# Two softmax attentions of a Trainium2 kernel: unscaled probabilities are multiplied, and a pair's outputs are scaled once

## The chip, the core and the metric

One NeuronCore of a Trainium2 chip runs the whole program in a single launch. The metric is the device time of a launch in microseconds; the median over three runs is compared. All matrix products and tiles are fp32 (128 partitions; TensorE writes to PSUM banks of 128x512 fp32).

## What is computed

The program is three transformer layers over 512 tokens of width 1024. Each of the first two has an attention with 12 token heads and 4 heads over 256 memory rows, all of width 64. The change touches the softmax attentions of these two layers:

```python
# layer 0: windowed attention with a sink
s = einsum('bqkgd,bskd->bkgqs', q_blk, k_blk) * scale + bias
s = where(valid, s, NEG)
p = softmax(concatenate([s, sink_l], axis=-1), axis=-1)[..., :SPAN]
out = einsum('bkgqs,bskd->bqkgd', p, v_blk)
# layer 1: neighbourhood attention on an 8 x 64 grid
s = einsum('bwhd,brwchd->bhwrc', q_row, k_nb) * scale + bias
p = softmax(s.reshape(B, B_HEADS, GRID_W, kr * kc), axis=-1)
out = einsum('bhwrc,brwchd->bwhd', p, v_nb)
# both layers, behind their 12 heads: memory attention
s = einsum('bshd,bmhd->bhsm', q, mk) * HEAD_DIM ** -0.5
p = softmax(s, axis=-1)
out = einsum('bhsm,bmhd->bshd', p, mv)
```

The output goes through a dense projection (`w_out`), a norm and an MLP. The third layer has other attentions; its dilated one runs through the same functions as "phase 2" and keeps its form.

## The kernel before

Every engine has its own program, written out by hand in plain loops; they meet at semaphores only. The order in which an engine works is the order of its code, and a wait holds back all that stands behind it on that engine.

The attention of phase 0 (layer 0) and phase 1 (layer 1) is a list of 32 steps: 8 pairs of heads (6 pairs of token heads, 2 of memory heads), for each pair 4 tiles of 128 queries. A step has two halves, one for each head. A window step has 257 or 385 columns (256 or 384 keys and one for the sink), in the order 257, 385, 385, 257 within a pair; a grid step has 192, 256, 256, 192; a memory step 256. I call the pairs window, grid and memory pairs.

The engines run a software pipeline over s, the number of the step:

- TensorE (`softmax` in its program, L2067): scores of step s into two of four banks (L2095); then `turn` (L2044) transposes the probabilities of step s-3 into one pair of banks, in pieces of 64x128 (8 transposes for 2 blocks of keys, 12 for 3; L2061); then the products with the values of step s-4 (L2139), which add up 128 columns of the pair's output bank. That bank, 64 rows a head and 512 queries, is full behind the fourth step. Scores wait for the masks of step s-2, `turn` for ScalarE's copy of the turn before.
- VectorE (L1260): the mask and row minimum of step s (L1301, two instructions and their accumulator reads), which needs the scores; then, for step s-1, it waits for the exponentials, takes the reciprocals of the two row sums (L1318, 128x2) and multiplies both halves of the probabilities in place (L1323). At the end of a pair it writes `o_lo`, the remainder of the output behind ScalarE's rounded `o_hi` (L1277), one iteration after that cast.
- ScalarE (L847): the copy of the turned probabilities of step s-3 from PSUM to `pt_short` (`copy_turned`, L816, L823), the exponentials of step s with their row sums (`exps`, L826, L834), and at the end of a pair the cast of the output bank to `o_hi` (`copy_output`, L838, L845).
- GpSimd loads the bias tiles of the pairs two pairs ahead, behind the masks that read the old ones.

In the first steps TensorE also makes part of the values, and behind step 31 (`n` is 32) it fills its waits with the first matmuls of the output projection (`begin_out`). The order of these three bodies is what sets the order of the work around the change: there is no scheduler. Banks 4 and 5 (`turn_banks`) take the transposes, banks 6 and 7 the outputs of alternating pairs.

## Time and profile before

| | us |
|---|---|
| median of 3 runs (1914.45 to 1915.96) | 1915.92 |
| the profiled execution | 1916.02 |
| its span | 1914.2 |
| TensorE busy | 1896.0 (99%) |
| VectorE busy | 963.2 (50%) |
| ScalarE busy | 772.5 (40%) |
| GpSimd busy | 182.6 (10%) |

The span is the time from the first to the last instruction on the core; the profiled execution's own time is 1.8 us more. Durations in the rows are those of this one execution. In rows, PE is TensorE (PEld its weight loads), DVE is VectorE, ACT is ScalarE, POOL is GpSimd, SP the engine that issues most loads. Neighbouring instructions of an engine overlap at their ends by some tens of nanoseconds, so the distance from start to start is shorter than a duration. Phase 0 lies at about 84 to 150 us of the span, phase 1 at about 672 to 742.

### The profile page before, as it was taken

The numbers are of one execution on the slowest core, as the hardware profiler recorded it, in microseconds if no ns is written. First come the engines' busy times: TensorE is split into PE (matmuls) and PEld (weight loads), VectorE is DVE, ScalarE is ACT, GpSimd is POOL, SyncE is SP. The second block draws the span as 40 slices with busy tenths as digits, with TensorE's granted clock in tenths as the row PEclk, the third lists the DMA queues.
The fourth block names the chain that finished last, engine by engine and source line by source line (L and its number), as shares of the span: only waits on it lengthen the run. The fifth ranks groups of instructions, "written<-read, shape, count | busy, mean of one in ns | idle before, by whom it ended". The sixth has DMA issues, their size and how long they took to land.

```text
span 1914.2 us, 25105 instructions
## 1 busy us (share of the span) xinstructions
PE 1896.0 (99%) x10458; PEld 1566.7 (82%) x10458; DVE 963.2 (50%) x1497; ACT 772.5 (40%) x1251; POOL 182.6 (10%) x196
## 2 busy tenths in 40 slices
PE   9999999999999999999999999999999999999998
PEld 7878888888888867888888888878887888888887
DVE  5693665553245274566553236443655555325532
ACT  5494433333333285433323324333764443212321
POOL 4112200000005041300000103000000020000000
PEclk9999999999999999999999999999999999999999
DMA  6512233334333311223333332331212333233222
GB/s 191 197 35 77 78 99 99 96 93 143 92 106 117 99 46 56 88 91 97 99 99 91 102 105 99 99 111 57 61 37 86 116 90 97 99 99 97 92 98 88
DMA packets 54136, 182.96 MB, mean 96 GB/s; under 512 B 6604, under 2 KB 10060, under 8 KB 53512
## 3 DMA queue, kind: packets, MB, share of 16 engines
q1 hardware_dynamic: 51528, 172.28, 28.6%
q0 software_dynamic: 2352, 9.02, 1.6%
q8 instruction: 83, 1.36, 0.3%
q14 instruction: 29, 0.24, 0.0%
q10 hardware_dynamic: 144, 0.06, 0.0%
HBM read 176.58 MB, written 4.76 MB: 95 GB/s over the span
## 4 chain that ended last, share of the span: by engine, by line
PE 88%; ACT 4%; DVE 4%; issue 1%; DMA 1%; POOL 1%; SPq 0%; DVEq 0%; ACTq 0%
PE bank L1889 22%; PE bank L1891 22%; PE bank L1890 22%; PE bank L1908 2%; PE bank L1909 2%; PE bank L1910 2%; ACT prob_long L834 1%; PE bank L2139 1%; ACT pt_short L823 1%; PE bank L1669 1%; PE bank L1672 1%; PE bank L1677 1%; PE bank L1968 1%; PE bank L1967 1%; PE bank L1969 1%
## 5 line engine op out<-in xcount | busy, mean ns | idle before, releaser
L1141 DVE TENSOR_TENSOR w_lo<-w_raw,w_hi 128x1024 fp32r<-128x1024 f32 (+3 forms) x319 | 388.2, 1219 | 710.4 <-ACT w_hi L647 710.2
L647 ACT CAST w_hi<-w_raw 128x1024 fp32r<-128x1024 f32 (+3 forms) x319 | 321.9, 1010 | 552.2 <-DMA w_raw<-in_w_down 131.6
L1889 PE MATMUL bank<-h_hi,w_hi 128*128 128x512 f32 x1272 | 496.4, 390 | 0.8 <-DVE w_lo L1141 0.5
L1890 PE MATMUL bank<-h_lo,w_hi 128*128 128x512 f32 x1272 | 495.7, 390 | 0.0
L1891 PE MATMUL bank<-h_hi,w_lo 128*128 128x512 f32 x1272 | 495.7, 390 | 0.0
L1889 PEld LDWEIGHTS bank<-h_hi,w_hi 128*128 128x128 f32 x1272 | 239.2, 188 | 52.9 <-issue 2.2
L1891 PEld LDWEIGHTS bank<-h_hi,w_lo 128*128 128x128 f32 x1272 | 239.2, 188 | 50.2
L1890 PEld LDWEIGHTS bank<-h_lo,w_hi 128*128 128x128 f32 x1272 | 239.1, 188 | 49.3
L1889 PE MATMUL bank<-a_hi,w_hi 128*128 128x512 f32 (+1 forms) x676 | 261.5, 387 | 0.0
L1890 PE MATMUL bank<-a_lo,w_hi 128*128 128x512 f32 (+1 forms) x676 | 261.3, 387 | 0.0
L1891 PE MATMUL bank<-a_hi,w_lo 128*128 128x512 f32 (+1 forms) x676 | 261.3, 386 | 0.0
L1891 PEld LDWEIGHTS bank<-a_hi,w_lo 128*128 128x128 f32 x676 | 127.0, 188 | 25.9
L1889 PEld LDWEIGHTS bank<-a_hi,w_hi 128*128 128x128 f32 x676 | 127.0, 188 | 25.9 <-DVE a_lo L1542 0.3
L1890 PEld LDWEIGHTS bank<-a_lo,w_hi 128*128 128x128 f32 x676 | 127.0, 188 | 25.8
L536 POOL COPY sq_sum<-sq 128x512 f32<-128x512 f32 x6 | 4.1, 685 | 1047.8 <-ACT sq L686 1047.8
L937 ACT CAST a_hi<-raw 128x512 fp32r<-128x512 f32 x44 | 27.3, 621 | 133.8 <-DVE raw L1424 133.8
L539 POOL TENSOR_TENSOR sq_sum<-sq_sum,sq 128x512 f32<-128x512 f32 x35 | 50.4, 1440 | 263.4 <-ACT sq L686 263.4
L834 ACT ACTIVATE prob_long<-prob_long,low_stat 128x256 f32<-128x256 f32 (+3 forms) x128 | 66.0, 527 | 7.0 <-DVE low_stat L1301 6.8
L934 ACT ACTIVATE act_out<-act_out 128x512 f32<-128x512 f32 x44 | 27.8, 632 | 92.8 <-DVE act_out L1419 92.8
L1419 DVE TENSOR_TENSOR act_out<-bank,rstd 128x512 f32<-128x512 f32 x44 | 48.5, 1103 | 11.8 <-ACT rstd L702 11.7
L1101 ACT CAST a_hi<-raw 128x512 fp32r<-128x512 f32 x32 | 19.9, 621 | 83.9 <-DVE raw L1583 83.9
L1908 PE MATMUL bank<-h_hi,w_hi 128*128 128x512 f32 x128 | 52.5, 410 | 0.0
(328 smaller groups left out, 2550.5 us busy)
## 6 DMA issues: line engine op xcount, KB each, us to landing
w_raw<-in_w_gu SPq DMA_DIRECT2D x87, 512.0 KB, 3.5
w_raw<-in_w_mlp_in SPq DMA_DIRECT2D x32, 512.0 KB, 3.5
w_raw<-in_w_mlp_out SPq DMA_DIRECT2D x32, 512.0 KB, 3.6
w_raw<-in_w_down SPq DMA_DIRECT2D x32, 448.0 KB, 3.3
w_raw<-in_w_out SPq DMA_DIRECT2D x24, 512.0 KB, 3.5
w_raw<-in_w_down SPq DMA_DIRECT2D x16, 512.0 KB, 3.5
w_raw<-in_w_gates SPq DMA_DIRECT2D x16, 512.0 KB, 3.5
w_raw<-in_w_qk_b SPq DMA_DIRECT2D x14, 512.0 KB, 3.6
```

The costliest lines, as they stand in the source:

```text
L539: made = nc.gpsimd.tensor_tensor(sq_sum[:, :], sq_sum[:, :], sq[:, c % 2, :], ALU.add)
L647: nc.scalar.copy(hi_of(v), raw_of(v)).then_inc(w_hi_done, 1)
L834: nc.scalar.activation(part, part, ACT.Exp, bias=top, scale=-1.0, accum_out=sums[:, s % 4, half, k:k + 1]).then_inc(p_exp, 1)
L934: nc.scalar.activation(act_out[:, p, :], act_out[:, p, :], ACT.Silu).then_inc(act_done, 1)
L1141: nc.vector.tensor_tensor(lo_of(v), raw_of(v), hi_of(v).bitcast(F32), ALU.subtract).then_inc(w_split, 1)
L1419: nc.vector.tensor_tensor(dst, of, reordered(layer, raw[:, p, :], rstd[:, :])[1], ALU.mult).then_inc(acc_read_dve, 1)
L1889: mm(acc, w1, hi, start=start, stop=False)
L1890: mm(acc, w1, lo, start=False, stop=False)
L1891: last = mm(acc, w2, hi, start=False, stop=end)
L1908: mm(ps[7][:, :], w1, hi, start=c == 0, stop=False)
L1909: mm(ps[7][:, :], w1, lo, start=False, stop=False)
L1910: last = mm(ps[7][:, :], w2, hi, start=False, stop=c == DC - 1)
```

## The change

Four things change in phases 0 and 1:

1. The transposes wait for the exponentials alone (`p_exp`), and what is transposed and multiplied with the values is not normalised. VectorE's reciprocals of 128x2 and its multiplications of the probabilities are gone from these phases.
2. Every row sum of a pair lands at a place of its own. Behind the exponentials of a pair's fourth step VectorE takes one reciprocal of 128x512, in which each of the eight sums (four query tiles, two heads) is read 64 times over, into the tile `raw`.
3. With the transposes of the next pair's first step TensorE transposes these reciprocals too (8 more), so that they lie as the output does; ScalarE's copy of that turn takes 8 blocks, 1024 columns, in place of 4. A turn and a copy of the reciprocals alone stand behind the last step (d == 32).
4. ScalarE's cast of the output is gone. VectorE, five steps later (s = d + 5, d the fourth step of the pair), behind the masks of step s and behind the reciprocal of the pair that has just ended, multiplies the output bank by the turned reciprocals into `act_out`, casts this to `o_hi`, and subtracts for `o_lo`, each waiting for the one before.

```diff
@@ -443,6 +442,13 @@
         attention = [window_steps(), grid_steps(), dilated_steps()]
 
         pt_bufs = [pt_short, pt_short, pt_dil]
+        def turned_blocks(phase, d, steps):
+
+            begin, end = 0, 2 * len(steps[d].blocks) if d < len(steps) else 4
+            if phase < 2 and d and d % 4 == 0:
+                begin, end = 0 if d < len(steps) else 4, 8
+            return begin, end
+
         LAG_T, LAG_V, PROB_RING = (3, 3, 2), (4, 4, 3), (4, 4, 3)
 
         def prob_of(phase, s, half):
@@ -816,10 +822,12 @@
             def copy_turned(phase, d, steps):
                 if d >= 2:
                     act.wait_ge(pv_done, pv[0] + d - 1)
+                if phase < 2 and d % 4 == 2 and d > 2:
+                    act.wait_ge(o_scaled, scaled[0] + d // 4)
                 act.wait_ge(t_ready, turned[0] + 1)
-                n = 2 * len(steps[d].blocks)
-                dst = pt_of(phase, d)[:, :P * n].rearrange("p (n r q) -> p r n q", n=n, r=2)
-                src = turn_banks[:, :, :64 * n].rearrange("p r (n q) -> p r n q", n=n)
+                begin, end = turned_blocks(phase, d, steps)
+                dst = pt_of(phase, d)[:, P * begin:P * end].rearrange("p (n r q) -> p r n q", n=end - begin, r=2)
+                src = turn_banks[:, :, 64 * begin:64 * end].rearrange("p r (n q) -> p r n q", n=end - begin)
                 nc.scalar.activation(dst, src, ACT.Copy).then_inc(pt_copied, 1)
                 turned[0] += 1
 
@@ -831,17 +839,16 @@
                     for k, both in enumerate(st.pieces):
                         p = both[half]
                         part = prob_of(phase, s, half)[:, p["at"]:p["at"] + p["width"]]
+                        of = st.pair_no % 2 if phase < 2 else k
                         nc.scalar.activation(part, part, ACT.Exp, bias=top, scale=-1.0,
-                                             accum_out=sums[:, s % 4, half, k:k + 1]).then_inc(p_exp, 1)
+                                             accum_out=sums[:, s % 4, half, of:of + 1]).then_inc(p_exp, 1)
                 masked[0] += 2 * m
 
             def copy_output(phase, d, steps, o_hi):
                 if not steps[d].last:
                     return
                 act.wait_ge(pv_done, pv[0] + d + 1)
-                dst, src = o_hi[:, steps[d].pair, :], bank_in(phase, 6 + steps[d].pair_no % 2)[:, :]
-                if phase == 2:
-                    dst, src = unclassed(dst, src)
+                dst, src = unclassed(o_hi[:, steps[d].pair, :], bank_in(phase, 6 + steps[d].pair_no % 2)[:, :])
                 nc.scalar.copy(dst, src).then_inc(o_hi_done, 1)
 
             def softmax(phase, o_hi, beside=None, last_values=None, read=None):
@@ -853,12 +860,10 @@
                     if s == 2 and last_values:
                         values_by_tile(last_values, *read)
                     if phase < 2:
-                        if 0 <= s - LAG_T[phase] < n:
+                        if 0 <= s - LAG_T[phase] <= n:
                             copy_turned(phase, s - LAG_T[phase], steps)
                         if s < n:
                             exps(phase, s, steps[s])
-                        if 0 <= s - LAG_V[phase] < n:
-                            copy_output(phase, s - LAG_V[phase], steps, o_hi)
                         if last_values and s >= n:
                             hi_to(last_values[1] + 2 + min(s - n, 2))
                     else:
@@ -1268,12 +1275,21 @@
                         return
                     st = steps[d]
                     o_count[0] += 1
+                    acc = bank_in(phase, 6 + st.pair_no % 2)[:, :]
+                    if phase < 2:
+                        dve.wait_ge(pt_copied, turned[0] + d + 2)
+                        dve.wait_ge(pv_done, pv[0] + d + 1)
+                        o = act_out[:, st.pair_no % 2, :]
+                        nc.vector.tensor_tensor(o, acc, pt_of(phase, d + 1)[:, 4 * P:8 * P], ALU.mult).then_inc(o_scaled, 1)
+                        dve.wait_ge(o_scaled, o_count[0])
+                        nc.vector.tensor_copy(o_hi[:, st.pair, :], o).then_inc(o_hi_done, 1)
+                        dve.wait_ge(o_hi_done, o_count[0])
+                        nc.vector.tensor_tensor(o_lo[:, st.pair, :], o, o_hi[:, st.pair, :].bitcast(F32),
+                                                ALU.subtract).then_inc(o_ready, 1)
+                        return
                     dve.wait_ge(o_hi_done, o_count[0])
-                    dst, src = o_lo[:, st.pair, :], bank_in(phase, 6 + st.pair_no % 2)[:, :]
-                    lead = o_hi[:, st.pair, :].bitcast(F32)
-                    if phase == 2:
-                        lead = unclassed(lead, src)[0]
-                        dst, src = unclassed(dst, src)
+                    lead = unclassed(o_hi[:, st.pair, :].bitcast(F32), acc)[0]
+                    dst, src = unclassed(o_lo[:, st.pair, :], acc)
                     nc.vector.tensor_tensor(dst, src, lead, ALU.subtract).then_inc(o_ready, 1)
 
                 for s in range(n + LAG_V[phase]):
@@ -1306,21 +1322,21 @@
                                 masked[0] += 1
                     d = s - 1
                     if 0 <= d < n:
-                        m, i = len(steps[d].pieces), d % 4
-                        expd[0] += 2 * m
-                        dve.wait_ge(p_exp, expd[0])
-                        total = sums[:, i, :, 0]
-                        if m > 1:
-                            nc.vector.tensor_reduce(den[:, i, :], sums[:, i, :, :m], axis=AX.X, op=ALU.add).then_inc(den_done, 1)
-                            dens[0] += 1
-                            dve.wait_ge(den_done, dens[0])
-                            total = den[:, i, :]
-                        nc.vector.reciprocal(rden[:, i, :], total).then_inc(rden_done, 1)
-                        rdens[0] += 1
-                        dve.wait_ge(rden_done, rdens[0])
-                        for half in range(2):
-                            part = prob_of(phase, d, half)[:, :steps[d].width]
-                            nc.vector.tensor_scalar(part, part, rden[:, i, half:half + 1], None, ALU.mult).then_inc(p_ready, 1)
+                        expd[0] += 2
+                        if phase < 2 and steps[d].last:
+                            dve.wait_ge(p_exp, expd[0])
+                            of = steps[d].pair_no % 2
+                            total = sums[:, :, :, of:of + 1].rearrange("p i h o -> p (i h) o").to_broadcast([P, 8, HD])
+                            nc.vector.reciprocal(raw[:, of, :].rearrange("p (n d) -> p n d", n=8), total).then_inc(rden_done, 1)
+                            rdens[0] += 1
+                        elif phase == 2:
+                            dve.wait_ge(p_exp, expd[0])
+                            nc.vector.reciprocal(rden[:, d % 4, :], sums[:, d % 4, :, 0]).then_inc(rden_done, 1)
+                            rdens[0] += 1
+                            dve.wait_ge(rden_done, rdens[0])
+                            for half in range(2):
+                                part = prob_of(phase, d, half)[:, :steps[d].width]
+                                nc.vector.tensor_scalar(part, part, rden[:, d % 4, half:half + 1], None, ALU.mult).then_inc(p_ready, 1)
                     if phase < 2:
                         output_remainder(s - LAG_V[phase] - 1)
                         if last_values and s >= n:
@@ -1333,9 +1349,10 @@
                         read(s, ps[7], beside.after(s))
                 if phase < 2:
                     output_remainder(n - 1)
-                turned[0] += n
-
-            masked, expd, dens, rdens, o_count, turned = [0], [0], [0], [0], [0], [0]
+                turned[0] += n + 1 if phase < 2 else n
+                pv[0] += n
+
+            masked, expd, rdens, o_count, turned, pv = [0], [0], [0], [0], [0], [0]
 
             def bias_load(phase, pair, half):
 
@@ -2045,14 +2062,14 @@
 
                 if d == 0:
                     wait_reads((act_read, 0, 0))
-                if not 0 <= d < len(steps):
+                if not (0 <= d < len(steps) or phase < 2 and d == len(steps)):
                     return
-                blocks = steps[d].blocks
                 if turned[0]:
                     pe.wait_ge(pt_copied, turned[0])
-                for half in range(2):
+                for half in range(2 if d < len(steps) else 0):
+                    blocks = steps[d].blocks
                     ready[0] += 1
-                    pe.wait_ge(p_ready, ready[0])
+                    pe.wait_ge(p_exp if phase < 2 else p_ready, ready[0])
                     first_key = steps[d].pieces[0][half]["first_key"]
                     for kt, (first, w) in enumerate(blocks):
                         keys = slice(first_key + first, first_key + first + w)
@@ -2061,12 +2078,21 @@
                             last = nc.tensor.transpose(ps[4 + part][:w, at_:at_ + 64],
                                                        prob_of(phase, d, half)[rows(part), keys],
                                                        ident[rows(part), 64 * part:64 * part + 64])
+                if phase < 2 and d and d % 4 == 0:
+                    pe.wait_ge(rden_done, heads[0] + d // 4)
+                    for i in range(4):
+                        for part in range(2):
+                            last = nc.tensor.transpose(ps[4 + part][:, 256 + 64 * i:256 + 64 * i + 64],
+                                                       raw[rows(part), (d // 4 - 1) % 2, P * i:P * i + P],
+                                                       ident[rows(part), 64 * part:64 * part + 64])
                 last.then_inc(t_ready, 1)
                 turned[0] += 1
 
             def softmax(phase, beside=None, rhs=None, after=None, last_values=None, st_out=None):
                 steps = attention[phase]
                 n = len(steps)
+                if phase == 2:
+                    ready[0] = 0
                 if last_values:
                     us, hi, lo, tiles, reads = last_values
                     begin_side()
@@ -2118,9 +2144,10 @@
                             wait_reads((n_act[0], 0, 0))
                         copied[0] += 1
                         pe.wait_ge(pt_copied, copied[0])
-                        banks = 1 if phase == 2 else 2
-                        if st.first and st.pair_no >= banks:
-                            pe.wait_ge(o_ready, heads[0] + st.pair_no - banks + 1)
+                        if st.first and phase < 2 and st.pair_no >= 2:
+                            pe.wait_ge(o_scaled, heads[0] + st.pair_no - 1)
+                        elif st.first and phase == 2 and st.pair_no:
+                            pe.wait_ge(o_ready, heads[0] + st.pair_no)
                         n_v = len(st.vs[0])
                         for x in range(n_v):
                             for half in range(2):
@@ -2151,6 +2178,8 @@
                     if phase == 2:
                         turn(phase, s - LAG_T[phase], steps, n_act[0])
                 heads[0] += steps[-1].pair_no + 1
+                if phase < 2:
+                    copied[0] += 1
 
             scored, ready, turned, copied, heads = [0], [0], [0], [0], [0]
 
```

VectorE's order in phase 0 before (L1301 is the mask, ISA its name here; a pair's last two steps and the next pair's first ones):

```order
L1318 RECIPROCAL rden<-sums 128x2
L1323 TENSOR_SCALAR prob_long<-prob_long,rden 128x385 x2
L1301 ISA prob_long,low_stat<-bank,bias_window 128x257
L1301 ISA low_stat 128x1
L1301 ISA prob_long,low_stat<-bank,bias_window 128x257
L1301 ISA low_stat 128x1
L1318 RECIPROCAL rden<-sums 128x2
L1323 TENSOR_SCALAR prob_long<-prob_long,rden 128x257 x2
L1277 TENSOR_TENSOR h_lo<-bank,h_hi 128x512
L1301 ISA prob_long,low_stat<-bank,bias_window 128x385
L1301 ISA low_stat 128x1
```

The same place after the change (L1317 is the mask, L1330 the reciprocal, L1283 to L1287 the output of the pair before):

```order
L1317 ISA prob_long,low_stat<-bank,bias_window 128x257
L1317 ISA low_stat 128x1
L1317 ISA prob_long,low_stat<-bank,bias_window 128x257
L1317 ISA low_stat 128x1
L1330 RECIPROCAL raw<-sums 128x512
L1283 TENSOR_TENSOR act_out<-bank,pt_short 128x512
L1285 CAST h_hi<-act_out 128x512
L1287 TENSOR_TENSOR h_lo<-act_out,h_hi 128x512
L1317 ISA prob_long,low_stat<-bank,bias_window 128x385
L1317 ISA low_stat 128x1
```

The small reciprocals and multiplications between masks are gone, and once in four steps four instructions of 512 columns stand in a row ahead of the masks of 385 columns.

ScalarE's order around the end of a pair, before (L823 the copy of a turn, with its blocks of 64 as the third number; L834 the exponentials):

```order
L834 ACTIVATE prob_long,sums<-prob_long,low_stat 128x385 x2
L823 ACTIVATE pt_short<-bank 128x2x4x64
L834 ACTIVATE prob_long,sums<-prob_long,low_stat 128x257 x2
L845 CAST h_hi<-bank 128x512
L823 ACTIVATE pt_short<-bank 128x2x6x64
L834 ACTIVATE prob_long,sums<-prob_long,low_stat 128x257 x2
```

And after:

```order
L843 ACTIVATE prob_long,sums<-prob_long,low_stat 128x385 x2
L831 ACTIVATE pt_short<-bank 128x2x8x64
L843 ACTIVATE prob_long,sums<-prob_long,low_stat 128x257 x2
L831 ACTIVATE pt_short<-bank 128x2x6x64
L843 ACTIVATE prob_long,sums<-prob_long,low_stat 128x257 x2
```

The copy ahead of the pair's last exponentials is twice as wide, and the cast behind them is gone.

TensorE's order at the same place after the change (L2078 the transposes of probabilities, L2085 those of reciprocals, L2166 the products with the values, L2121 the scores); before, the row of L2085 is not there and the rest stands as it does:

```order
L2121 MATMUL bank<-k_buf,q_buf 128x256 x2
L2078 MATMUL bank<-ident,prob_long 128x64 x8
L2085 MATMUL bank<-ident,raw 128x64 x8
L2166 MATMUL bank<-pt_short,v_buf 64x128 x4
L2121 MATMUL bank<-k_buf,q_buf 128x256 x2
```

The eight transposes of reciprocals lie between a pair's ordinary transposes and the products with the values.

## Rows read from the trace of the kernel before

**Rows 1.** The page's busy times: us, share of the span, instructions

```profile
PE 1896.0 (99%) x10458; PEld 1566.7 (82%) x10458; DVE 963.2 (50%) x1497; ACT 772.5 (40%) x1251; POOL 182.6 (10%) x196
```

**Rows 2.** Timeline, ScalarE, one window pair: start us, us, what, [idle before]

```profile
102.46 0.58 ACT L845 CAST h_hi<-bank 128x512 fp32r<-128x512 f32 x1
102.92 0.82 ACT L823 ACTIVATE pt_short<-bank 128x768 f32<-128x768 f32 x1
...
104.61 0.81 ACT L823 ACTIVATE pt_short<-bank 128x768 f32<-128x768 f32 x1
105.30 0.63 ACT L834 ACTIVATE prob_long<-prob_long,low_stat 128x385 f32<-128x385 f32 x1
...
106.50 0.60 ACT L823 ACTIVATE pt_short<-bank 128x512 f32<-128x512 f32 x1
...
109.64 0.59 ACT L845 CAST h_hi<-bank 128x512 fp32r<-128x512 f32 x1
```

**Rows 3.** Timeline, ScalarE: casts that bound the six periods, and two grid steps

```profile
144.46 0.58 ACT L845 CAST h_hi<-bank 128x512 fp32r<-128x512 f32 x1
...
689.56 0.56 ACT L845 CAST h_hi<-bank 128x512 fp32r<-128x512 f32 x1
...
715.00 0.50 ACT L834 ACTIVATE prob_long<-prob_long,low_stat 128x256 f32<-128x256 f32 x1
...
715.99 0.58 ACT L823 ACTIVATE pt_short<-bank 128x512 f32<-128x512 f32 x1
716.47 0.45 ACT L834 ACTIVATE prob_long<-prob_long,low_stat 128x192 f32<-128x192 f32 x1
...
717.34 0.57 ACT L845 CAST h_hi<-bank 128x512 fp32r<-128x512 f32 x1
...
730.01 0.59 ACT L845 CAST h_hi<-bank 128x512 fp32r<-128x512 f32 x1
```

**Rows 4.** Timeline, VectorE and ScalarE: masks, remainder, who follows whom

```profile
104.48 0.55 DVE L1301 CUSTOM_DVE_ANT_0 prob_long<-bank,bias_window 128x385 f32<-128x385 f32 x1
...
705.41 0.67 DVE L1277 TENSOR_TENSOR h_lo<-bank,h_hi 128x512 fp32r<-128x512 f32 x1
706.00 0.41 DVE L1301 CUSTOM_DVE_ANT_0 prob_long<-bank,bias_grid 128x256 f32<-128x256 f32 x1
706.34 0.08 DVE L1301 DVE_READ_ACCUMULATOR2_ANT low_stat<- 128x1 f32 x1
...
706.45 0.51 ACT L834 ACTIVATE prob_long<-prob_long,low_stat 128x256 f32<-128x256 f32 x1 [0.61 <-DVE low_stat L1301]
...
730.16 0.17 DVE L1318 RECIPROCAL rden<-sums 128x2 f32<-128x2 f32 x1 [0.46 <-ACT prob_long L834]
```

**Rows 5.** Timeline, TensorE, one narrow step of a window pair

```profile
107.01 0.70 PE L2095 MATMUL bank<-k_buf,q_buf 64*128 64x256 f32 x4
107.54 0.41 PE L2061 MATMUL bank<-ident,prob_long 64*128 64x64 f32 x8
107.88 0.66 PE L2139 MATMUL bank<-pt_short,v_buf 128*64 128x128 f32 x8
108.47 0.49 PE L2095 MATMUL bank<-k_buf,q_buf 64*128 64x256 f32 x2
```

**Rows 6.** Groups by form, VectorE: operation, shapes, count | busy us, mean ns

```profile
L1277 DVE TENSOR_TENSOR h_lo<-bank,h_hi 128x512 fp32r<-128x512 f32 x16 | 10.9, 683 | 5.2 <-ACT h_hi L845 5.2
...
L1318 DVE RECIPROCAL rden<-sums 128x2 f32<-128x2 f32 x72 | 11.5, 160 | 0.9 <-ACT prob_long L834 0.8
...
L1497 DVE CAST sb_ql<-zero_bias 64x512 fp32r<-64x512 f32 x2 | 0.8, 422 | 0.1
...
L1365 DVE CAST neg_tri<-raw 128x128 fp32r<-128x128 f32 x1 | 0.2, 205 | 0.0
```

**Rows 7.** Timeline, TensorE, tail of phase 0: two turns

```profile
145.88 0.46 PE L2061 MATMUL bank<-ident,prob_long 64*128 64x64 f32 x8
...
147.10 0.46 PE L2061 MATMUL bank<-ident,prob_long 64*128 64x64 f32 x8 [0.16 <-ACT pt_short L823]
```

7 lines of the change are left out of this document (4 added, 3 removed).

## The prediction

> **What bounds the kernel now.** I read the page first: TensorE is busy 99% of the span [rows 1], so a microsecond lost or won on TensorE anywhere is one in the total. That average says nothing of the two attentions that the change touches, so next I read the timeline there, engine by engine. I call E the moment at which the exponentials of a pair's last step end; ScalarE then casts the output of the pair before, so each E is the start of a cast and can be read off.
>
> In the first attention, ScalarE's cast starts at 102.46 and again at 109.64 [rows 2]: 7.18 us for a pair of window heads, with no idle entry on any row between. ScalarE sets this period. The six periods from 102.46 to 144.46 take 42.00 us [rows 2, 3]. In the second attention the six from 689.56 to 730.01 take 40.45 us, 6.74 us each, though ScalarE's own work for a grid pair is 4 x 0.48 + 2 x 0.99 + 2 x 0.87 + 0.46 = 6.10: there it also waits for VectorE, as the row at 706.45 shows [rows 3, 4]. From start to start on ScalarE: two exponentials of 257 or 256 columns take 0.99 us, of 385 columns 1.20, of 192 columns 0.87, a copy of turned probabilities 0.48 for 512 columns and 0.69 for 768, the cast 0.46 [rows 2, 3].
>
> TensorE is close behind. A narrow step takes 1.46 us (107.01 to 108.47), of it 0.53 scores and 0.34 eight transposes [rows 5]: 5.84 us for four. VectorE has the masks, the reciprocals, the normalising and the remainder, and is nearly as full. So three engines are balanced, and what counts is less how much each has to do than in which order.
>
> **The change, part by part.** VectorE loses, in each of 64 steps, a reciprocal of 0.16 us and two multiplications of the probabilities. Since ScalarE sets the period in the first attention, this is worth nothing there; in the second it removes some waits of ScalarE.
>
> ScalarE loses 16 casts of 0.46 us and gains 16 copies that are 512 columns wider. From 512 to 768 columns the step grows by 0.21 [rows 2], so to 1024 by 0.42, and the copy takes 0.90 (no such copy of this stage is in the trace; the growth is a straight line between the two that are). Net zero.
>
> TensorE gains eight transposes per pair, 0.34 us, 16 times: 5.4 us of work. It lies under ScalarE's and VectorE's waits if these decide, and on the path if not. The wide copy also delays the next transposes. A turn with 512 columns behind it comes back after 1.22 us (145.88 to 147.10 [rows 7]); with 0.34 and 0.42 more, 1.98, while TensorE has 1.46 + 0.34 = 1.80 of other work. That would be a wait of 0.18 per pair.
>
> VectorE gains four operations per pair, and here the order decides. Once in four steps it waits for E, then runs in a row the reciprocal of 128x512, the multiplication that reads the bank, the cast, and the remainder. Only then come the masks of the next step, though their scores have long been ready, and ScalarE needs these masks for its next exponentials. The chain from E to those exponentials:
>
> - E to VectorE's start: 0.15 (730.01 to 730.16) [rows 3, 4].
> - Reciprocal of 512 columns: not in the trace. Bounds for the forecast are 0.42 below, what a one-input cast of 512 columns took, and 0.68 above; rival 1 takes up what lies far above. I take 0.68, what one 128x512 operation at one element a step costs (the remainder, 0.683) [rows 6]; 0.60 from start to start, since the remainder of 705.41 is followed at 706.00 [rows 4].
> - Multiplication reading the bank: 0.68, the same shape as the remainder, and 0.04 for the semaphore (0.03 at 706.42 to 706.45 [rows 4]).
> - Cast from SBUF to SBUF: 0.42 (0.422 for the same shape [rows 6]; at one element a step it would be 0.68, the upper bound), and 0.04.
> - Remainder: 0.60 to the next start.
> - First mask to its exponentials: 0.45 with 256 columns (706.00 to 706.45), 0.14 more with 385 (0.55 against 0.41) [rows 4].
>
> Sum: 2.98 us, 3.12 for window heads. Without the wait, ScalarE would come to these exponentials after one copy, two exponentials and one copy: 0.48 + 0.87 + 0.48 = 1.83 us behind E in the grid pairs, 1.95 in the memory pairs, 0.69 + 0.99 + 0.69 = 2.37 in the window pairs. So ScalarE stands still for 0.7 to 1.15 us in each pair, on exactly the work that was moved off it.
>
> From there to the next E ScalarE works without a gap: window 1.20 + 0.48 + 1.20 + 0.90 + 0.99 = 4.77; grid 0.99 + 0.48 + 0.99 + 0.90 + 0.87 = 4.23; memory 0.99 + 0.48 + 0.99 + 0.90 + 0.99 = 4.35. New periods: window 3.12 + 4.77 = 7.89, grid 2.98 + 4.23 = 7.21, memory 2.98 + 4.35 = 7.33. Each is longer than TensorE's own (5.84 + 0.34 + 0.18 = 6.36 for narrow pairs), so the added transposes lie under it.
>
> Each attention has six such periods: outputs of six pairs are scaled before the last masks, the other two behind them. First attention: 4 x 7.89 + 2 x 7.33 = 46.22 against 42.00, +4.2. Second: 4 x 7.21 + 2 x 7.33 = 43.50 against 40.45, +3.05. The first wide copy comes before the first of these periods, +0.4 in the first attention. In the tails, eight transposes more (+0.34 each) stand against a wide copy and exponentials that now lie beside the output projection's first matmuls; I take the two at -0.2 together, with bounds of -1.2 and +0.7. The pair's last remainder comes some 0.5 us later than now, under the projection's matmuls that TensorE has in hand.
>
> Waits that the change adds and that I cost at nothing: the transposes of the reciprocals wait for the reciprocal, issued three steps earlier; the copy that overwrites the turned reciprocals waits for the multiplication, ready at E + 1.4, when ScalarE gets there at E + 1.35 to 1.7; VectorE's wait for the turned reciprocals ended before E. No DMA is added. The bias tiles of GpSimd are released by VectorE's masks, which are not later than ScalarE's use of them.
>
> Sum: 4.2 + 3.05 + 0.4 - 0.2 = 7.5 us on the profiled execution's 1916.02, which is 0.1 above the median of the runs: 1923.5 by median.
>
> **The rule that speaks against the reciprocal.** The row: 128x2 took 0.160 us [rows 6]. With one element a step its bulk is fixed cost, as in the two-input operation, where 0.683 at 512 columns leaves about 0.16. The Trainium skill, "VectorE: DVE Perf Modes", section "First, the fixed hardware budget", says that the reciprocal is an iterative division with a repeat count of 8. If that meant eight passes for each element, an estimate from the slope of one-pass operations would be some 4.2 us for 512 columns, and the kernel would come to about 1971; the row of two elements can hardly tell eight passes from one.
>
> **Rivals.**
>
> 1. *The reciprocal is dear per element.* Plain casts took 0.205 at 128 columns and 0.422 at 512 [rows 6], so 0.135 for none; by that line, 0.160 for two elements leaves 12.5 ns for each, and 6.4 us for 512. The period is then 5.7 us longer, 12 times, and the first reciprocal of each attention costs about 4.9 (it too stands ahead of masks): 7.5 + 69 + 10 = 86, so 2002. Half of that price per element gives about 1957. Against it: the remainder's line, which makes two elements cost 0.16 with nothing left over. Chance 0.18.
>
> 2. *Not slower.* If masks come before ScalarE asks, because reciprocal, multiplication and cast together take 1 us less than I reckon or run where VectorE idles, then the relief of VectorE shows and TensorE sets the periods. The point from which it decides is a chain from E below 1.95 us. Window pairs would then go from 7.18 to about 7.55 (TensorE shows no idle there either and gains 0.52), narrow pairs to 6.36: first attention 4 x 0.37 and 2 x 6.36 against 13.28, +0.9; second 40.45 to 38.4, -2.1; with the 0.4, about -0.8, so 1915. For it: in the second attention ScalarE demonstrably waited for VectorE. Against it: the four operations are serial, each waits for the one before, and 0.42 + 0.68 + 0.42 + 0.60 is already above the mark with its ends. Chance 0.20, with what partly absorbs the wait.
>
> **How the numbers follow.** The forecast has 0.62: with a reciprocal of 0.42 it gives 1920.4, with a cast of 0.68 (0.26 more, 12 times) and the tails at their worst about 1927.5. A measurement of this kernel can tell some 0.2%, 3.8 us. Slower by more than that: most of the forecast's cases, 0.56, and rival 1, 0.18: 0.74. Same: 0.06 and nearly all of rival 2: 0.21. Faster: 0.05, if narrow pairs gain more than TensorE's rows allow me. The range takes in the forecast and rival 2 and leaves out rival 1: 1914 to 1930.
>
> **What would show it.** Right: in the profile after, a reciprocal of 128x512 near 0.68 us; ScalarE idle once a pair, for 0.7 to 1.2 us, released by VectorE's mask; E to E near 7.9, 7.2 and 7.3 us; VectorE's busy sum lower than before though the time is longer. Wrong: a reciprocal of microseconds (rival 1), or no idle on ScalarE behind the first step of a pair (rival 2), or TensorE's transposes as the engine everybody waits for.

## The result and the profile after

| | before | after |
|---|---|---|
| median of 4 runs each, us | 1915.94 (1914.45 to 1917.19) | 1965.83 (1965.68 to 1966.41) |
| ratio | | 1.0262, interval 1.0249 to 1.0275 |
| span of the profiled execution, us | | 1964.6 |
| E to E, first attention, window pairs | 7.18 | 10.51 |
| six periods of the first / second attention, us | 42.0 / 40.5 | 63.4 / 63.5 |

The kernel became 2.6% slower, where 0.4% was forecast (1923.5) and the range ended at 1930. The sign was right, the size wrong by a factor of more than six (49.9 us for 7.6).

The page, with the busy times of [rows 1], the granted clock over 40 slices, and the engines' shares of the chain that ended last:

```profile
PE 1923.4 (98%) x10586; PEld 1581.6 (81%) x10586; DVE 986.6 (50%) x1353; ACT 774.8 (39%) x1237; POOL 180.8 (9%) x196
...
PEclk9999999999999987999999999999999999999999
...
PE 88%; DVE 5%; ACT 4%; issue 3%; DMA 1%; SPq 0%; DVEq 0%; ACTq 0%
```

The page alone would hardly tell a reader what happened. It shows a clock dip in two slices and a chain that spends 88% of the span on TensorE, as before. The groups by form do tell it. These are the four operations of VectorE that the change adds (busy us, mean ns | idle before, what ended most of it), which answer to [rows 6]:

```profile
L1330 DVE RECIPROCAL raw<-sums 128x512 f32<-128x512 f32 x16 | 53.6, 3352 | 6.9 <-ACT prob_long L843 6.9
L1283 DVE TENSOR_TENSOR act_out<-bank,pt_short 128x512 f32<-128x512 f32 x16 | 10.2, 636 | 4.4 <-ACT pt_short L831 4.4
L1285 DVE CAST h_hi<-act_out 128x512 fp32r<-128x512 f32 x16 | 6.8, 427 | 0.6
L1287 DVE TENSOR_TENSOR h_lo<-act_out,h_hi 128x512 fp32r<-128x512 f32 x16 | 11.1, 693 | 0.5
```

The multiplication, the cast and the remainder cost nearly what the forecast took (0.68, 0.42, 0.68). The reciprocal of 128x512 takes 3.35 us where 0.68 was taken. Its place is seen in VectorE's timeline of one window pair (start us, us, what, [idle before]), to be laid beside [rows 4]:

```profile
115.13 3.35 DVE L1330 RECIPROCAL raw<-sums 128x512 f32<-128x512 f32 x1 [0.19 <-ACT prob_long L843]
118.40 0.63 DVE L1283 TENSOR_TENSOR act_out<-bank,pt_short 128x512 f32<-128x512 f32 x1
119.06 0.43 DVE L1285 CAST h_hi<-act_out 128x512 fp32r<-128x512 f32 x1
119.53 0.69 DVE L1287 TENSOR_TENSOR h_lo<-act_out,h_hi 128x512 fp32r<-128x512 f32 x1
120.13 0.55 DVE L1317 CUSTOM_DVE_ANT_0 prob_long<-bank,bias_window 128x385 f32<-128x385 f32 x1
...
125.64 3.35 DVE L1330 RECIPROCAL raw<-sums 128x512 f32<-128x512 f32 x1 [0.19 <-ACT prob_long L843]
```

The four run back to back, and the next mask stands behind all of them, 5.13 us after E, which is at 115.00. The second reciprocal starts 10.51 us after the first: that is the period. ScalarE, which had no idle entry in [rows 2], now has two within 1.7 us:

```profile
119.11 0.81 ACT L831 ACTIVATE pt_short<-bank 128x768 f32<-128x768 f32 x1 [2.33 <-DVE act_out L1283]
...
120.73 0.62 ACT L843 ACTIVATE prob_long<-prob_long,low_stat 128x385 f32<-128x385 f32 x1 [0.80 <-DVE low_stat L1317]
...
121.94 0.57 ACT L831 ACTIVATE pt_short<-bank 128x512 f32<-128x512 f32 x1
...
123.62 1.00 ACT L831 ACTIVATE pt_short<-bank 128x1024 f32<-128x1024 f32 x1
```

The 0.80 is the wait that the forecast named. The 2.33 is the wait of the copy that overwrites the turned reciprocals, which the forecast put at nothing. With a reciprocal of 3.35 the multiplication ends at 119.0, long after ScalarE has come. It costs nothing of its own, though: both waits end inside the same chain, and the second alone would end at the same moment. TensorE's row shows what reaches the engine on which the total is counted:

```profile
119.98 0.46 PE L2078 MATMUL bank<-ident,prob_long 64*128 64x64 f32 x8 [1.77 <-ACT pt_short L831]
```

One more thing is new, the granted clock. Windows of the kernel after (us, then busy us and count of PE, PEld, DVE, ACT and POOL, then PEclk, DMA share, GB/s), two stretches in the attentions and one outside:

```profile
143.00:149.00 6.00, 5.51 (x52) 4.24 (x52) 2.88 (x11) 5.09 (x15) 0.00 (x0) 0.50 0.00 0
724.00:733.00 9.00, 9.00 (x78) 5.90 (x74) 5.76 (x9) 4.59 (x15) 4.77 (x8) 0.50 0.10 29
172.00:600.00 428.00, 427.63 (x1954) 353.00 (x1953) 210.11 (x219) 157.33 (x198) 35.53 (x24) 1.00 0.32 99
```

At 0.50 TensorE is at its lower level, 1.2 GHz. There are two such stretches in the first attention and three in the second, 44 us in all, and before the change there were none in either. Each comes behind idle time of TensorE. The stretch from about 743.5 on, for instance, follows a wait of 2.20 us that ends at 742.20:

```profile
742.20 0.47 PE L2078 MATMUL bank<-ident,prob_long 64*128 64x64 f32 x8 [2.20 <-ACT pt_short L831]
```

**Where the 49.9 us are.** I compare the moments E of the two traces, each read off as the start of ScalarE's next instruction, as in the prediction. They add up as follows:

| part | us |
|---|---|
| 12 periods, as the forecast has them with a reciprocal of 0.68 | +7.3 |
| 12 periods, 3.35 instead of 0.68 for the reciprocal: 12 x 2.67 | +32.0 |
| 12 periods, the rest (63.39 + 63.47 less 82.45 before and the two lines above) | +5.1 |
| before the first of the six periods, both attentions: 2.03 + 1.75 | +3.8 |
| behind the last E of the first attention | +1.8 |
| sum | +50.0 |

The last E of the second attention is at 779.94 against 730.01, 49.9 later. The profiled executions differ by 50.4 us in the end (the medians by 49.9); where behind this E the other 0.5 arises I did not follow. In the first attention the rest, 1.2 us, lies where the clock is low: the three window periods at the full clock are 10.51, even 0.05 shorter than 7.89 + 2.67, while the fourth, with the beginning of a low stretch, takes 10.69, and the memory pair behind it 10.84 where 7.33 + 2.67 = 10.0 was due. The tail of the first attention shows the same. Its first nine matmuls of the output projection take 3.78 us (166.87 to 170.65), at the low clock up to about 170.5; before the change they took 2.29 (143.59 to 145.88). One of them, before and after:

```profile
143.93 0.40 PE L2041 MATMUL bank<-h_lo,w_hi 128*128 128x512 f32 x1
```

```profile
167.46 0.63 PE L2058 MATMUL bank<-h_lo,w_hi 128*128 128x512 f32 x1
```

So some 1.5 of the tail's 1.8 us are the low clock too.

### The profile page after: what moved, and what is told of

It reads as the page before. It is cut to its first block, busy times and chain, and to the rows that moved or that the text cites. A ratio compares the mean times of both kernels' runs of the same rounds, so it can differ in the third digit from the quotient of the medians.

```text
span 1964.6 us, 25223 instructions
## 1 busy us (share of the span) xinstructions
PE 1923.4 (98%) x10586; PEld 1581.6 (81%) x10586; DVE 986.6 (50%) x1353; ACT 774.8 (39%) x1237; POOL 180.8 (9%) x196
## 4 chain that ended last, share of the span: by engine, by line
PE 88%; DVE 5%; ACT 4%; issue 3%; DMA 1%; SPq 0%; DVEq 0%; ACTq 0%
PE bank L1906 21%; PE bank L1907 21%; PE bank L1908 21%; PE bank L1925 2%; PE bank L2166 2%; PE bank L1926 1%; PE bank L1927 1%; PE bank L2121 1%; ACT prob_long L843 1%; PE bank L2078 1%; PE bank L1686 1%; PE bank L1689 1%; PE bank L1694 1%; PE bank L1985 1%; PE bank L1984 1%
## 5 line engine op out<-in xcount | busy, mean ns | idle before, releaser
L1906 PE MATMUL bank<-h_hi,w_hi 128*128 128x512 f32 x1272 | 496.5, 390 | 0.8 <-DVE w_lo L1148 0.5
L944 ACT CAST a_hi<-raw 128x512 fp32r<-128x512 f32 x44 | 27.3, 621 | 133.7 <-DVE raw L1441 133.7
L2078 PEld LDWEIGHTS bank<-ident,prob_long 64*128 64x128 f32 x560 | 27.5, 155 | 48.2 <-ACT pt_short L831 44.3
L831 ACT ACTIVATE pt_short<-bank 128x512 f32<-128x512 f32 (+2 forms) x66 | 47.3, 716 | 47.3 <-DVE act_out L1283 27.0
L2078 PE MATMUL bank<-ident,prob_long 64*128 64x64 f32 x560 | 33.3, 248 | 26.1 <-ACT pt_short L831 26.0
```

The costliest lines, as they stand in the source:

```text
L831: nc.scalar.activation(dst, src, ACT.Copy).then_inc(pt_copied, 1)
L1906: mm(acc, w1, hi, start=start, stop=False)
L2078: last = nc.tensor.transpose(ps[4 + part][:w, at_:at_ + 64], prob_of(phase, d, half)[rows(part), keys], ident[rows(part), 64 * part:64 * p ...
```

## The experiments

Two theories stood after the result. **A:** it is the reciprocal's length and nothing else, so the rest of the chain was priced rightly. **B:** the order is at fault, and the wait of the masks behind the scaling would cost much even with a cheap reciprocal. Later runs ask what the relief of VectorE is worth and why it never showed.

### The sizes of a reciprocal

The kernel before, with eight operations put on VectorE at one place:

```
+for w in (8, 32, 128, 512):
+    nc.vector.reciprocal(act_out[:, 0, :w].rearrange("p (n d) -> p n d", n=8),
+                         ones[:, 0:8].rearrange("p (n o) -> p n o", o=1).to_broadcast([P, 8, w // 8]))
...
+for w in (8, 32, 128):
+    nc.vector.reciprocal(act_out[:, 1, :w], ones[:, :w])
...
+nc.vector.tensor_copy(act_out[:, 0, :].rearrange("p (n d) -> p n d", n=8),
+                      ones[:, 0:8].rearrange("p (n o) -> p n o", o=1).to_broadcast([P, 8, HD]))
```

> The kernel before with reciprocals on VectorE added in an early stretch: 8, 32, 128 and 512 columns with a source of 8 values each read over and over, 8, 32 and 128 columns with a plain source, and one copy of 8 values to 512 columns. Theory (a fixed part and six steps for each element, whatever the source): 0.20, 0.34, 0.95 and 3.35 us, plain ones the same at 8, 32 and 128, the copy 0.42 to 0.69. Rival (the repeated source is what costs): the plain ones at 128 columns take 0.3 us or less.

Groups by form; line 1363 reads each element w/8 times over, line 1368 reads plain columns:

```profile
L1363 DVE RECIPROCAL act_out<-ones 128x512 f32<-128x512 f32 x1 | 3.4, 3353 | 0.0
L1363 DVE RECIPROCAL act_out<-ones 128x128 f32<-128x128 f32 x1 | 1.0, 953 | 0.0
L1368 DVE RECIPROCAL act_out<-ones 128x128 f32<-128x128 f32 x1 | 1.0, 953 | 0.0
L1371 DVE COPY act_out<-ones 128x512 f32<-128x512 f32 x1 | 0.4, 427 | 0.0
...
L1368 DVE RECIPROCAL act_out<-ones 128x32 f32<-128x32 f32 x1 | 0.4, 353 | 0.0
...
L1368 DVE RECIPROCAL act_out<-ones 128x8 f32<-128x8 f32 x1 | 0.2, 203 | 0.0
```

From 128 to 512 columns: (3353 - 953) / 384 = 6.25 ns for each, and 953 - 128 x 6.25 = 153 ns fixed. By that line 32 columns are 353 and 8 are 203, as measured, and two are 0.166, close to the 0.160 of [rows 6]. That row has two columns, and so could not tell 6.25 ns from one. Reading one element again and again costs nothing more, where both forms were run (8, 32 and 128 columns); a copy that spreads eight elements over 512 columns takes 427 ns. So eight reciprocals and a copy do the same in 0.63 us, one duration added to the other.

### A small reciprocal in the same place

```
-nc.vector.reciprocal(raw[:, of, :].rearrange("p (n d) -> p n d", n=8), total).then_inc(rden_done, 1)
+nc.vector.reciprocal(rden[:, :, :], sums[:, :, :, of]).then_inc(small_done, 1)
+dve.wait_ge(small_done, smalls[0])
+few = rden[:, :, :].rearrange("p i (h o) -> p (i h) o", o=1).to_broadcast([P, 8, HD])
+nc.vector.tensor_copy(raw[:, of, :].rearrange("p (n d) -> p n d", n=8), few).then_inc(rden_done, 1)
```

> The changed kernel, but VectorE takes the reciprocals of the eight sums (128x8) and then copies each 64 times over into raw (128x512). Theory (only the price of the wide reciprocal was mis-sized; the order of VectorE's work stands as predicted): reciprocal and copy together take about 0.66 us, ScalarE stands idle behind the first step of each pair, periods 7.9 us (window), 7.2 (grid) and 7.3 (memory), and the time is 1923.5 us, 1921 to 1926, some 7.5 above the kernel before. Rival (the wide reciprocal was not most of it; transposes and wide copies on TensorE and ScalarE, or a lower granted clock, hold much of the 50 us): 1935 or more. Rival (the chain on VectorE costs nothing once the reciprocal is cheap): 1915.

Measured: 1925.80 (1923.23 to 1928.76) against 1915.24, ratio 1.0056, interval 1.0043 to 1.0068. This run is the kernel that the prediction described, with 0.58 us between the start of the reciprocal and that of the multiplication instead of the forecast's 0.60. VectorE, from its timeline (the third row is the multiplication, the last the first mask):

```profile
103.25 0.20 DVE L1330 RECIPROCAL rden<-sums 128x8 f32<-128x8 f32 x1
103.49 0.43 DVE L1334 COPY raw<-rden 128x512 f32<-128x512 f32 x1
103.83 0.68 DVE L1284 TENSOR_TENSOR act_out<-bank,pt_short 128x512 f32<-128x512 f32 x1
...
105.62 0.55 DVE L1318 CUSTOM_DVE_ANT_0 prob_long<-bank,bias_window 128x385 f32<-128x385 f32 x1
```

and ScalarE, the exponentials that this mask releases:

```profile
106.21 0.62 ACT L844 ACTIVATE prob_long<-prob_long,low_stat 128x385 f32<-128x385 f32 x1 [0.60 <-DVE low_stat L1318]
```

E is at 103.12, so the chain takes 3.09 (3.12 forecast) and the rest of the period 4.78 (4.77). The periods come out at 7.87, 7.88, 7.87, 7.87, 7.31 and 7.31 us where 7.89 and 7.33 were forecast. In the second attention they are 7.20 to 7.46, 43.9 us in all against 43.5. The low clock is gone from both attentions. Theory A explains 40 of the 50 us (with the low clock, which goes with the dear reciprocal), and B is right about the 10 that are left: even cheap, the scaling in front of the masks costs more than the change saves.

### The order alone, with a dear and with a cheap reciprocal

The same two versions, with the reciprocal (and in the second version its copy, as above) issued one step later, behind the next step's masks. The block leaves its place under `steps[d].last` for:

```
+if phase < 2 and 0 <= s - 2 < n and steps[s - 2].last:
+    dve.wait_ge(p_exp, expd[0] - (2 if s - 1 < n else 0))
+    of = steps[s - 2].pair_no % 2
...
```

> The changed kernel with its wide reciprocal (3.35 us) moved one step later, behind that step's masks and no longer ahead of the output's scaling. Theory (the 50 us are the reciprocal's length times its place in the chain from E to the next masks): the chain from E loses the reciprocal, but the masks of the step after now wait for it; VectorE's own work is 8.3 us for a window pair and 7.5 to 7.8 for the others, ScalarE still waits about 2 us a pair: periods 8.3 to 9 us against 10.5 and 9.9, time 1940 us (1930 to 1948). Rival (only the length counts, not the place): 1960 to 1966.

Measured for the dear one: 1947.02 (1945.20 to 1947.34) against 1915.23, ratio 1.0162, interval 1.0146 to 1.0177. The time is near the upper end of what was expected, and the window period, 9.20, just above it (8.3 to 9). VectorE spends 37.0 of 40 us busy there (33.8 in the kernel after), more than any other engine.

```profile
116.24 3.35 DVE L1338 RECIPROCAL raw<-sums 128x512 f32<-128x512 f32 x1
119.50 0.50 DVE L1317 CUSTOM_DVE_ANT_0 prob_long<-bank,bias_window 128x385 f32<-128x385 f32 x1
```

The reciprocal now holds up the masks of the step behind: ScalarE waits 1.93 us for them, and TensorE's turn of the reciprocals 0.56. Moving it gets back 19 of the 50 us, not more. The low clock stays in the second attention (0.82 between 720 and 740 us), so the 32 us that remain are not the order's alone.

> As e1, and reciprocal and copy moved one step later, behind that step's masks. The scaling of the output then no longer stands behind the wait for the exponentials. Theory: the multiplication starts as soon as the turned reciprocals are copied, about 1 us before E; the masks of the next step are ready before ScalarE asks; TensorE or ScalarE sets the periods: 7.2 to 7.6 us window, 6.3 to 6.5 grid and memory, time 1915 (1913 to 1918). Rival (what costs is the four operations' length, wherever they stand): 1920 or more. ScalarE's idle time before its exponentials should fall to that of the kernel before or less.

Measured for the cheap one: 1917.47 (1915.55 to 1920.48) against 1915.24, ratio 1.0013, interval 1.0004 to 1.0021. The window period is 7.39. TensorE now sets it: its timeline has no idle entry in such a pair, while VectorE waits for scores in two of a pair's four steps and ScalarE's own work is 0.25 us shorter than the period; the row that TensorE has more than before is the turn of the reciprocals:

```profile
115.33 0.41 PE L2083 MATMUL bank<-ident,prob_long 64*128 64x64 f32 x8
115.57 0.42 PE L2090 MATMUL bank<-ident,raw 64*128 64x64 f32 x8
115.92 0.66 PE L2171 MATMUL bank<-pt_short,v_buf 128*64 128x128 f32 x8
```

It moves the start of the next matmuls by 0.35 us, and the period is 0.21 longer than before the change. With this order the change costs hardly more than can be measured, but it still wins nothing.

### What the relief of VectorE is worth

The kernel before, with no reciprocals and no multiplications in the first two attentions, so that their outputs stay unscaled:

```
-if 0 <= d < n:
+if 0 <= d < n and phase == 2:
...
-pe.wait_ge(p_ready, ready[0])
+pe.wait_ge(p_exp if phase < 2 else p_ready, ready[0])
```

> The kernel before without the reciprocals and the multiplications of the probabilities in the first two attentions (their outputs stay unscaled), nothing added: what the relief of VectorE alone is worth. Theory (ScalarE sets the first attention, VectorE held up only the second): six periods of the first attention stay at 42.0 us; those of the second fall from 40.45 to about 38; time 1913.5 (1912.5 to 1915). Rival (VectorE was the bound of both): 1910 or less. Rival (worth nothing): 1915.9.

Measured: 1911.93 (1909.91 to 1913.79) against 1915.24, ratio 0.9983, interval 0.9973 to 0.9992. That is a little below the expected 1912.5 to 1915. All of it lies in the second attention: its last six periods become 6.10 to 6.32 us, in the grid pairs ScalarE's own 6.10, and 37.1 in all instead of 40.5, while those of the first stay as they were (7.17 to 7.19 in the window pairs). So about 3.3 us is the most that taking this work from VectorE could bring, before any price for doing it elsewhere. ScalarE keeps its cast in this run, so what the relief of ScalarE is worth is not in it.

### What the turned reciprocals cost

The small reciprocal issued later, without the transposes and with narrow copies; the outputs are multiplied by reciprocals that were not transposed:

```
-if phase < 2 and d and d % 4 == 0:
-    begin, end = 0 if d < len(steps) else 4, 8
+if phase < 2 and d == len(steps):
+    begin, end = 4, 8
...
-nc.vector.tensor_tensor(o, acc, pt_of(phase, d + 1)[:, 4 * P:8 * P], ALU.mult)
+nc.vector.tensor_tensor(o, acc, raw[:, st.pair_no % 2, :], ALU.mult)
```

> As e2, but the reciprocals are not transposed (except behind the last step) and the turns' copies keep their former width; the output is multiplied by the reciprocals as they lie, so its values are others. Theory (e2's 5.5 us over the kernel without normalising are TensorE's added transposes, 7.39 = 7.04 + 0.34 in the window pairs, and the wait for the wide copy): 1912 (1911 to 1913.5), window periods 7.2 at most, grid 6.1 to 6.4. Rival (VectorE's scaling of the output is what costs in e2): 1917 as e2.

Measured: 1913.99 (1913.13 to 1916.05) against 1915.24, ratio 0.9993, interval 0.9984 to 1.0002. That is 3.5 us below the version with the transposes, and just above the expected 1911 to 1913.5. The window period falls from 7.39 to 7.0, once 7.25. Of the 5.5 us between that version (1917.47) and the one without any normalising (1911.93), the transposes with their wide copies are 3.5. The other 2.1 are the net of two effects, which the six periods of each attention show. In the first they take 41.2 us here against 42.0 without any normalising: ScalarE, which set the pace there, has no cast any more. In the second they take 40.0 against 37.1: three operations of VectorE stand ahead of masks again, and ScalarE waits 3.3 us for masks between 690 and 728 us, where it had no such wait.

### The second attention alone

Since the relief is worth something only there, this run leaves the first attention as it was before the change, and issues the small reciprocal later in the second. Each branch of the change gets the second attention's phase alone, and the first its output copy on ScalarE again:

```
-if phase < 2 and d and d % 4 == 0:
+if phase == 1 and d and d % 4 == 0:
     begin, end = 0 if d < len(steps) else 4, 8
...
+if phase == 0 and 0 <= s - LAG_V[phase] < n:
+    copy_output(phase, s - LAG_V[phase], steps, o_hi)
```

> As e2 (small reciprocals, one step later), in the second attention only; the first is as in the kernel before. Theory (in the first attention ScalarE's 7.18 us is nearly TensorE's 7.04, so 0.34 us of transposes costs; in the second VectorE held the period): the first attention as before (periods 7.19), the second as in e2 (6.5 to 6.6 with one longer): 1915.24 + 0 - 1 = 1914.3 (1913 to 1916), 3 us below e2. Rival (the gain of e2's second attention was chance): 1915.2 or more.

Measured: 1916.56 (1914.67 to 1918.61) against 1915.23, ratio 1.0004, interval 0.9995 to 1.0012. The expectation of 1914.3 missed: the second attention takes 40.7 us for its six periods, against 40.5, as the rival expectation (1915.2 or more) had it. VectorE and then ScalarE in one pair:

```profile
717.56 0.69 DVE L1288 TENSOR_TENSOR act_out<-bank,pt_short 128x512 f32<-128x512 f32 x1
718.28 0.43 DVE L1290 CAST h_hi<-act_out 128x512 fp32r<-128x512 f32 x1
718.74 0.69 DVE L1292 TENSOR_TENSOR h_lo<-act_out,h_hi 128x512 fp32r<-128x512 f32 x1
719.35 0.42 DVE L1324 CUSTOM_DVE_ANT_0 prob_long<-bank,zero_bias 128x256 f32<-128x256 f32 x1
```

```profile
719.81 0.51 ACT L844 ACTIVATE prob_long<-prob_long,low_stat 128x256 f32<-128x256 f32 x1 [0.47 <-DVE low_stat L1324]
```

Even without the reciprocal, the other three operations hold the masks for 1.8 us, and ScalarE waits 0.47. So the next two runs spread these three over two steps (cast and remainder one step later), first in the second attention, then in both:

```
+def output_parts(d):
...
+    nc.vector.tensor_copy(o_hi[:, st.pair, :], o).then_inc(o_hi_done, 1)
...
+if phase == 1:
+    output_parts(s - LAG_V[phase] - 2)
```

> As e7 (second attention only), but VectorE casts the scaled output and writes its remainder one step later, behind that step's masks; beside the masks of step d + 5 only the multiplication stands. Theory (in e7 ScalarE still stands idle 0.5 us a pair, since multiplication, cast and remainder take 1.8 us between two steps' masks; split, none of them is waited for): periods of the second attention from 6.78 us to 6.4 on the mean, time 1914.3 (1913 to 1915.5). Rival (TensorE's added 0.34 us and the wait for the wide copy hold it, not VectorE): 1916.5, periods unchanged.

Measured: 1917.56 (1916.44 to 1920.00) against 1915.65, ratio 1.0011, interval 1.0003 to 1.0020. It missed again, and is no better than the run that it was to mend. The wait is still there, one step on: now cast, remainder, reciprocal and copy stand together (720.30 to 721.94), and the masks behind them release ScalarE at

```profile
722.40 0.51 ACT L844 ACTIVATE prob_long<-prob_long,low_stat 128x256 f32<-128x256 f32 x1 [0.51 <-DVE low_stat L1330]
```

> As e2 (both attentions), with the same split. Theory: window periods stay at TensorE's 7.39 us, the memory and grid pairs fall to 6.4 or so: 1915.5 us (1914.5 to 1917), 2 us below e2 and no better than the kernel before. Rival: 1917.5 as e2.

Measured: 1920.21 (1918.24 to 1923.35) against 1915.65, ratio 1.0029, interval 1.0017 to 1.0041. Another miss: the window period grows from 7.39 to 7.63. Spreading the pieces made it worse in the first attention, where ScalarE had hardly waited for a mask before. Now it does in each window pair, behind the same four operations as in the run above (cast, remainder, reciprocal and copy, 113.52 to 115.16):

```profile
115.76 0.62 ACT L844 ACTIVATE prob_long<-prob_long,low_stat 128x385 f32<-128x385 f32 x1 [0.35 <-DVE low_stat L1324]
```

### The low clock

The kernel after, with TensorE making the first scores of every fourth step three times, so that it works through part of its wait:

```
+for again in range(2 if phase < 2 and s >= 8 and s % 4 == 2 else 0):
+    for half, p in enumerate(both):
+        of, first, w, q, k = p["scores"][0]
+        mm(bank_in(phase, (scored[0] + half) % 4)[of, first:first + w], q, k, start=True, stop=True)
```

> The changed kernel, but TensorE makes the scores of every fourth step three times over in its long wait (same values, 1.5 us of work where it waited 1.8). Theory (stretches at half the granted clock, 41 us of them in the changed kernel, follow TensorE's idle time and cost about 6 us on top of the chain): the stretches within the two attentions vanish, periods go from 10.7 to 9.95 (memory) and from 10.7 to 9.9 (every second grid pair), time 1960 us (1958 to 1962). Rival (the clock does not matter, TensorE is hidden): 1965.8 unchanged. Rival (the added matmuls are on the path): 1970 or more.

Measured: 1964.61 (1964.43 to 1965.03) against 1915.23, ratio 1.0253, interval 1.0239 to 1.0267. Windows of this run, where the kernel after had 0.50 in both:

```profile
143.00:149.00 6.00, 5.28 (x80) 3.87 (x82) 4.04 (x11) 5.26 (x16) 0.00 (x0) 1.00 0.01 3
722.00:732.00 10.00, 10.00 (x78) 7.01 (x76) 6.26 (x12) 5.43 (x18) 4.75 (x8) 0.50 0.10 28
```

In the first attention the low stretches are gone, and its last two periods fall from 10.84 and 10.33 to 9.93 and 9.95, where 7.33 + 2.67 = 10.0 was due. So there the idle time of TensorE brought the clock down, and the clock made the difference, 1.5 us over the six periods. In the second attention two of the three stretches remain, with periods up to 11.2 us. The added scores of a grid pair are shorter (0.97 us against 1.40 in a window pair) and leave a wait of 1.61 us (at 719.52) where a window pair keeps 0.48 (at 130.45). A memory pair of the first attention keeps 1.58 without a low stretch behind it, so why the clock still fell in the second stays open. These two stretches are most of why the run came out at 1964.6 and not at 1960.

## Why the prediction was wrong, point by point

- **The reciprocal, the step that failed.** "I take 0.68, what one 128x512 operation at one element a step costs." It takes 3.35, 0.15 fixed and 6.25 ns for each column. The slope of one-pass operations, (0.422 - 0.205) / 384 = 0.57 ns for the cast or (0.683 - 0.16) / 512 = 1.02 for the two-input one [rows 6], was borrowed from operations that do another kind of work. Rival 1 had the mechanism at chance 0.18, with prices of 12.5 ns an element and half of it, 6.25, which is what was measured. For that half it gave 1957 (by its own terms it is nearer 1959), still some 7 to 9 us short, for the clock most of all. What I held against it, that two elements at 0.16 have nothing left over above the remainder's fixed 0.16, could not decide it: 2 x 6.25 = 12.5 ns is all that there was to see, and the fixed costs of two kinds of operation need not agree to that.
- **The rule beside it.** The measured slope of 6.25 ns is six times the 1.02 ns of a one-pass two-input operation. The Trainium skill, "VectorE: DVE Perf Modes", section "First, the fixed hardware budget", gives a repeat count of 8. Read as eight passes at 1.02 ns, that was my estimate of 4.2 us and 1971. Measured were 3.35 and 1965.8, so the trace does not bear out eight such passes, but it is much nearer to them than to my term. No row spoke against a dear slope, and the chance should have moved from the forecast to rival 1.
- **The chain from E to the next exponentials: right but for that term.** With reciprocal and copy at 0.58 the chain of a window pair took 3.09 us for a forecast of 3.12, and the periods were 7.87 and 7.31 for 7.89 and 7.33. The profiled execution was 8.0 us longer than that of before for a forecast of 7.5; by the medians it is 10.6. The places of the wait, the engine that waits and the releaser were as forecast (0.60 idle in the window pair, 0.72 from start to start, 0.75 forecast).
- **The wide copy: right.** It is 1.00 us busy and 0.90 to the next start (123.62 to 124.52), as forecast.
- **Transposes under other waits: right for the forecast order,** and in the kernel after. It does not hold once these waits are gone: with the wide copies they then cost 3.5 us.
- **Waits at nothing.** The copy over the turned reciprocals did wait, 2.3 us a time in the window pairs (27 us in all), because the reciprocal was longer than the forecast. It ends inside the same chain.
- **First parts and tails.** Both first parts grew by about 2 us (2.03, 1.75), where +0.4 stood for one. The first reciprocal of each attention stands ahead of masks too; rival 1 had seen this. The tail of the first attention lost 1.8 us where -0.2 was taken for both, outside the bounds of -1.2 and +0.7; some 1.5 of it are matmuls at the low clock, which no term had.
- **Not foreseen: the clock.** A dear reciprocal leaves TensorE idle for some 2 us a pair, and it then runs at 1.2 GHz for a while. In the periods that is at most the 5.1 us of the rest, with the tail's 1.5 some 6.5. The run that filled the waits shows 1.5 us of the periods; for the second attention, 4 us, the share of the clock is argued and not shown, and 0.4 of it stands in the run with the small reciprocal too, at the full clock.
- **Rival 2, not slower.** It needed a chain from E below 1.95 us, 2.37 in window pairs, and the forecast order never had it. With the small reciprocal behind the masks the exponentials of a window pair start 2.46 us after E (110.60 to 113.06), so ScalarE hardly waits, and the outcome is near this rival's: 1917.5 with the window period at 7.39, where it reckoned 1915 and 7.55. The gain that it expected in narrow pairs, 2 us, did not show: the scaling itself still stands before masks.

## What to carry to other kernels

The price of an operation that works several passes per element cannot be read from a row with two elements; if the nearest row has two columns where 512 are asked for, and no row speaks against a dear slope, the dear case deserves most of the chance, or the operation should be made small. Take reciprocals before spreading them: 128x8 and a copy to 128x512 are 0.63 us, the reciprocal of the spread 128x512 is 3.35. And before work is moved off an engine, run the kernel without it: here that bounds the gain from VectorE's relief at 3.3 us, and the transposes with their wide copies alone cost 3.5. Taking the cast from ScalarE, which set the first attention's pace, was worth another 0.8 us there.

## What the runs showed of the hardware

- VectorE's reciprocal: 203, 353, 953 and 3353 ns for 8, 32, 128 and 512 fp32 columns, so 153 ns and 6.25 ns a column. A plain source and one read repeatedly are alike at 32 and 128 columns, and within 7 ns at 8; the 512 were run with a repeated source only.
- VectorE's copy of eight elements spread over 512 columns takes 427 ns, as a cast of 512 plain columns does (0.422 [rows 6]).
- TensorE's granted clock fell to 0.50 in five stretches of the two attentions, when TensorE stood still for about 2 us in each pair of some 10; in the run with the small reciprocal in place, whose waits there were at most 0.5 us (39.1 of 40 us busy), it stayed at 1.00. In the kernel after, between 104 and 144 us, TensorE was busy for 30.0 of 40 us and the clock still at 0.99.
- At 0.50 a matmul of 128x512 in the output projection took 0.63 us, at 1.00 it took 0.40.
